# Two blocks of a bidirectional token mixer: who builds and sums the first two levels of a recurrence, and on how many rows and columns of TensorE

## The reference, cut to what matters

```python
scores = jnp.einsum('bhtsd,bhsd->bhts', qb[:, :, :, None, :] * decay, kb)   # decay = exp(cum_t - cum_s), s <= t
o = scores @ vb + (qb * jnp.exp(cum)) @ s
s_new = jnp.exp(last[:, :, 0, :])[..., None] * s + jnp.einsum('bhsd,bhse->bhde', kb * jnp.exp(last - cum), vb)
```

## Time and profile before

| | before |
| --- | --- |
| median of 3 runs | 3790.6 us (3789.75 to 3802.39) |
| the profiled execution | 3798.3 us, its span 3796.5 us |
| TensorE busy | 3503.6 us, 92% of the span |
| VectorE busy | 2010.7 us, 53% |
| ScalarE busy | 1149.5 us, 30% |
| mean granted TensorE clock | 0.965 |

### The profile page before, as it was taken

How to read it: one execution, slowest core, us unless ns; L and a number is a source line. 1 busy time by engine, 2 the same in 40 slices (tenths; PEclk the granted TensorE clock), 3 DMA queues, 4 the chain that set the end, 5 groups by cost and what they waited for, 6 DMA issues and landing times.

```text
span 3796.5 us, 50206 instructions
## 1 busy us (share of the span) xinstructions
PE 3503.6 (92%) x18584; PEld 2837.3 (75%) x18584; DVE 2010.7 (53%) x3025; ACT 1149.5 (30%) x1620; POOL 1003.3 (26%) x412
## 2 busy tenths in 40 slices
PE   6799999898889999999888889999999988989998
PEld 2388888787777777777677657788888767668887
DVE  5766341538844368783467575644331466762112
ACT  1221212344421123222433264321212332543222
POOL 2133223321121144444210101223223211123443
PEclk9899999999999999999989899999999988899999
DMA  5233332321132135453110101233322211112222
GB/s 197 94 125 129 123 111 78 132 67 34 40 107 64 52 116 174 172 174 107 62 67 23 56 17 34 99 111 133 122 103 66 77 40 34 45 44 84 94 94 94
DMA packets 101863, 341.46 MB, mean 90 GB/s; under 512 B 10159, under 2 KB 21551, under 8 KB 100240
## 3 DMA queue, kind: packets, MB, share of 16 engines
q1 hardware_dynamic: 82760, 301.90, 23.4%
q10 hardware_dynamic: 18952, 37.51, 2.8%
HBM read 325.21 MB, written 14.16 MB: 89 GB/s over the span
## 4 chain that ended last, share of the span: by engine, by line
issue 76%; POOL 19%; DMA 1%; PE 1%; DVE 1%; POOLq 0%; ACT 0%; ACTq 0%; SPq 0%; DVEq 0%
POOL wr_lo L2355 19%; PE ps L1259 1%; DMA raw<-in_stream 0%; DMA hyena_k<-fst 0%; PE ps L1266 0%; DVE mod_out L539 0%; DMA raw<-in_mod_stream 0%; PE ps L410 0%; POOLq L2354 0%; POOLq L2351 0%; DVE fnorm L1398 0%; ACTq L1319 0%; DVE H L740 0%; POOL wr_lo L2348 0%; PE ps L438 0%
## 5 line engine op out<-in xcount | busy, mean ns | idle before, releaser
L2355 POOL TENSOR_TENSOR wr_lo<-raw,wr_hi 128x1024 fp32r<-128x1024 f32 x388 | 970.0, 2504 | 2642.2 <-ACT wr_hi L494 2642.1
L410 PE MATMUL ps<-xx_hi,wr_hi 128*128 128x512 f32 x1728 | 689.1, 399 | 6.8 <-DVE H L900 5.7
L410 PE MATMUL ps<-xx_hi,wr_lo 128*128 128x512 f32 x1728 | 683.4, 395 | 0.0
L410 PE MATMUL ps<-xx_lo,wr_hi 128*128 128x512 f32 x1728 | 681.7, 395 | 0.0
L494 ACT ACTIVATE wr_hi<-raw 128x1024 fp32r<-128x1024 f32 x388 | 411.5, 1061 | 590.9 <-PE ps L410 309.0
L539 DVE CUSTOM_DVE_ANT_0 ps<-raw,cb 128x1024 f32<-128x1024 f32 x240 | 400.3, 1668 | 56.0 <-DMA raw<-in_mod_stream 25.8
L850 DVE TENSOR_TENSOR ff_raw<-ps,ff_gate 128x768 f32<-128x768 f32 (+1 forms) x88 | 72.6, 825 | 657.8 <-PE ps L410 650.3
L410 PEld LDWEIGHTS ps<-xx_hi,wr_hi 128*128 128x128 f32 x1728 | 326.6, 189 | 86.3 <-DVE H L900 6.5
L410 PEld LDWEIGHTS ps<-xx_lo,wr_hi 128*128 128x128 f32 x1728 | 326.6, 189 | 73.8 <-issue 2.1
L410 PEld LDWEIGHTS ps<-xx_hi,wr_lo 128*128 128x128 f32 x1728 | 326.3, 189 | 72.2
L900 DVE SCALAR_TENSOR_TENSOR H<-ps,hgv,H 128x512 f32 (+3 forms) x168 | 106.1, 659 | 285.5 <-PE ps L438 150.0
(11 more groups left out here) (383 smaller groups left out, 6193.9 us busy)
## 6 DMA issues: line engine op xcount, KB each, us to landing
raw<-in_stream SPq DMA_DIRECT2D x392, 512.0 KB, 3.3
raw<-in_mod_stream SPq DMA_DIRECT2D x168, 512.0 KB, 4.3
hK<-hyena_k ACTq DMA_DIRECT2D x4, 1152.0 KB, 6.0
h_kept<-H ACTq DMA_DIRECT2D x2, 2048.0 KB, 9.0
hyena_k<-fst ACTq DMA_DIRECT2D x14, 256.0 KB, 11.2
H<-in_h ACTq DMA_DIRECT2D x1, 3072.0 KB, 15.5
h_kept<-H ACTq DMA_DIRECT2D x1, 3072.0 KB, 9.9
H<-h_kept ACTq DMA_DIRECT2D x1, 3072.0 KB, 9.8
```

Source lines behind the costliest of these rows:

```text
L410: last = pe.matmul(gslot(slot)[:, col:col + n], w, rhs[part], start=(bi == 0 and pi == 0), stop=(bi == len(blocks) - 1 and pi == 2))
L2355: nc.gpsimd.tensor_tensor(wr_lo[:, s, :], raw[:, s % RAW, :], wr_hi[:, s, :], ALU.subtract).then_inc(tile_lo, 1)
```

## The change

ACT takes over the copies of levels 0 and 1 into `u_P`, block by block and with no mask: one copy of 64 key rows at level 0, two of 32 rows at level 1. ACT makes the copy of level li after its exponential of level li+2. DVE leaves out both masked copies and waits, before it copies level 2, for ACT's copy of level 1. At level 0 PE scores only the 64 key rows that are used. With two heads in a unit, the chunk sums (L968) become two products of 64 columns, one for each head, packed in 64 columns of features; the state `u_S` is 64 wide, its mask is gone, and the product with it in the output stage (L1003) reads the 64 feature rows of its own head. DVE waits for the `u_Z` of the level before, ahead of the exponents two levels on.

```diff
             for c in order[:5]:
-                last = pe.matmul(m[:, c * P:(c + 1) * P], U["ktok"][:, c * P:(c + 1) * P], vt(c),
-                                 start=True, stop=True)
+                for j in range(nsub):
+                    f = slice(j * P // nsub, (j + 1) * P // nsub)
+                    last = pe.matmul(m[f, c * P:c * P + P // nsub], U["ktok"][:, c * P + f.start:c * P + f.stop],
+                                     vt(c)[:, f], start=True, stop=True)
...
-                        last = pe.matmul(m[:, j * NX + c * HD:j * NX + (c + 1) * HD], Z[r, c * CH:(c + 1) * CH],
+                        keys = (slice(HD, P) if bw else slice(0, HD)) if li == 0 else slice(0, P)
+                        last = pe.matmul(m[keys, j * NX + c * HD:j * NX + (c + 1) * HD],
+                                         Z[r, c * CH + keys.start:c * CH + keys.stop],
                                          queries[r, c * per:(c + 1) * per, 0 if bw else 1, :], start=True, stop=True)
...
                     if at_order > 0:
-                        last = pe.matmul(m[f, cc], U["S"][:, at_order, f], U["eq"][:, cc], start=False, stop=True,
-                                         skip_group_check=True)
+                        last = pe.matmul(m[f, cc], U["S"][f, at_order, 0:P // nsub], U["eq"][f, cc],
+                                         start=False, stop=True, skip_group_check=True)
...
+        def act_put(act, tally, U, li, nsub, toks, ms, done, read):
+            b, bw, nch = LEVELS[li], U["bw"], toks // CH
+            act.wait_ge(misc_done, done)
+            for n in range(HD // b):
+                keys = slice((2 * n + bw) * b, (2 * n + bw + 1) * b)
+                queries = (2 * n + 1 - bw) * b
+                dst = U["P"].rearrange("p j (c t) -> p j c t", t=CH)[keys, :, :, queries:queries + b]
+                src = mslot(ms).rearrange("p (j c t) -> p j c t", j=2, t=HD)[keys, 0:nsub, 0:nch, n * b:(n + 1) * b]
+                ins = act.activation(dst, src, ACT.Copy)
+                if n < HD // b - 1:
+                    ins.then_inc(act_step, 1)
+                    act.wait_ge(act_step, tally.next("act_step"))
+            ins.then_inc(misc_free[ms], 1)
+            act.wait_ge(misc_free[ms], read)
...
+                if li in BLOCK_LEVELS:
+                    return
+                if li - 1 in BLOCK_LEVELS:
+                    dve.wait_ge(misc_free[tally.place("misc_done", 2)], tally.read("misc_done", 2))
...
-                src = add[:, c * P:(c + 1) * P]
-                if nsub == 2:
-                    src = U["Z"][:, 1, c * P:(c + 1) * P]
-                    dve.tensor_tensor(src, add[:, c * P:(c + 1) * P], blk[:, :], ALU.mult).then_inc(dve_step, 1)
-                    dve.wait_ge(dve_step, tally.next("dve_step"))
-                dst = U["S"][:, n_ + 1, :]
+                src = add[:, c * P:c * P + P // nsub]
+                dst = U["S"][:, n_ + 1, 0:P // nsub]
...
                 if li + 2 < nl:
+                    dve.wait_ge(z_ready, tally.now("z_ready", -2))
                     dve_seam(dve, tally, U, li + 2, toks)
```

More of the change, by code:

```diff
@@ L37 @@
 LEVELS = (64, 32, 16, 8, 4, 2, 1)
+BLOCK_LEVELS = (0, 1)
 RING = 4
@@ L1036, in act_unit @@
             tally.passed("misc_done", nsub + 1)
+            at_level = []
             for li in range(len(LEVELS)):
@@ L1039, in act_unit @@
                     act_level(act, tally, U, li, toks, scale)
-                tally.passed("misc_done")
+                at_level.append((tally.take("misc_done"), tally.now("misc_done"), tally.read("misc_done")))
+                if li - 2 in BLOCK_LEVELS:
+                    act_put(act, tally, U, li - 2, nsub, toks, *at_level[li - 2])
                 ahead(li)
             tally.passed("misc_done")
+        def act_put(act, tally, U, li, nsub, toks, ms, done, read):
[12 more added lines that the diff above has]
+            act.wait_ge(misc_free[ms], read)
         def dve_cum(dve, tally, U):
@@ L1143, in dve_unit @@
                 else:
-                    ins = dve.scalar_tensor_tensor(out=dst, in0=U["S"][:, n_, :], scalar=U["dec"][:, c:c + 1], in1=src,
+                    ins = dve.scalar_tensor_tensor(out=dst, in0=U["S"][:, n_, 0:P // nsub], scalar=U["dec"][:, c:c + 1], in1=src,
                                                    op0=ALU.mult, op1=ALU.add)
```

## The result

| | before | after |
| --- | --- | --- |
| median | 3795.9 us (4 runs, 3789.8 to 3802.4) | 3844.8 us (4 runs, 3839.2 to 3845.6) |
| the profiled execution, its span | 3796.5 us | 3843.8 us |
| mean granted TensorE clock | 0.965 | 0.954 |

The changed kernel is slower: the ratio is 1.0125, with a 95% interval of 1.0102 to 1.0149. The forecast was 3807 us (3771 to 3830).

The account below looks back on a forecast made before the run. TensorE, busy for 92% of the span, was taken as the bound. Row changes +36, waits -11.5, TensorE's own work -1.5 and clock -7 gave +16 us on 3790.6: 3807 us, range 3771 to 3830.

Parts of the forecast that it names:

- The price of a row change: Output stage: alternating 128*64 and 64*64 tiles cost 0.36 us per two instructions, 1.0 us more a chunk, 36 us in all.
- The first rival: Output stage: the two tile shapes take turns freely, with no drain, giving 3771 us; chance 0.17.
- The clock term: TensorE's clock dips behind the waits that the change removes would go too: 7 us off, 10 at most.
- The sign of being wrong: B units: the prediction is wrong if their mean clock moves by more than 0.05.
- The third rival: Behind unit ends: drains are paid and one or two more long low-clock stretches add 10 to 20 us, about 3825; chance 0.17.
- Waits ahead of level 1: B units: level 1's u_Z comes 1.9 us sooner, ending TensorE's waits there; all B-unit waits together 11.5 us off.
- ScalarE in A units: A units: ScalarE's level 0 copy delays its level 3 exponential, leaving VectorE 0.16 us gained instead of 0.9.
- the next step: A units: the 0.16 us gain is lost at GpSimd's subtraction, so 0 counted, between -7 and +3 us.
- TensorE's own work: Level 0 with half the weights and narrower chunk sums: 1.5 us off, from nothing to 5, over all units.

Follow-up runs that it names:

- second: The kernel before with one edit, the state product L1003 reading only its own head's 64 feature rows: 3857.3 us, ratio 1.0170.
- fourth: The kernel before with the second recurrence's output stage issued three times over, dense and of one tile shape: 3826.4 us, ratio 1.0094.
- seventh run: The kernel before with only ScalarE's copies of levels 0 and 1 and the 64 keys of level 0: 3790.1 us, ratio 0.9986.
- third run: The changed kernel with each chunk's u_P products of both heads before its u_S products, halving the row-size changes: 3794.6 us, ratio 1.0007.

## Why the prediction was wrong

**The price of a row change** was right. The step of two instructions was put at 0.36 us and measures 0.36 at 2.4 GHz, and so do its two parts: of the two in 0.43 us the last takes 0.27, so it starts 0.16 behind the first, which leaves 0.20 for the change. The 0.16 had no row behind it in the forecast, so that it fits is in part luck. At full clock the stage takes 7.7 us against 2.7 in the last unit of the first layer, 5.0 more for five chunks as counted, and 5.8 against 2.0 in that of the second, 3.8 more for four. The first rival (tiles that take turns freely) is out. By the rule that the section on the output stage cites from the Trainium skill ("TensorEngine Tiling (Array Packing)", Key Properties) the change from 128*64 to 64*64 drains the engine; the trace agrees, with 0.36 us for a run of two instructions where it was 0.11.

**The clock term failed**: "I count 7" off, with the opposite left to a rival of "one or two long stretches". The sign of being wrong that the prediction named for it came too: the mean clock of the second B unit moved by 0.14, where 0.05 was the mark. TensorE's busy time in the two stages can be read from windows, before and after:

```profile
1932.70:2119.33 186.63, 167.21 (x1404) 143.13 (x1404) 146.41 (x228) 54.31 (x65) 17.51 (x8) 0.89 0.07 23
3061.14:3213.89 152.75, 135.09 (x956) 107.65 (x956) 116.97 (x220) 47.24 (x65) 17.08 (x7) 0.84 0.08 28
```

```profile
1926.97:2148.77 221.80, 204.92 (x1444) 157.60 (x1444) 132.62 (x200) 61.41 (x77) 19.06 (x8) 0.77 0.06 22
3090.62:3259.75 169.13, 156.51 (x996) 111.72 (x996) 104.46 (x192) 52.62 (x77) 18.93 (x8) 0.76 0.08 26
```

Busy time goes from 302.3 to 361.4 us, 59 more. The row changes at full clock are 4 x 5.0 + 4 x 3.8 = 35 of it, and level 0 takes off 4 x 0.63 + 4 x 0.43 = 4. The remaining 28 us are put down to the lower clock. Idle time falls from 37.1 to 29.5 us. So the clock term was +28 and not -7. These 35 us are more than the whole distance of 31 between the forecast of +16 and the +47 of the two spans; the other terms together come to -3 (waits +4, row changes -1, level 0 -3, A units -4, in whole us). The prediction had seen that an output stage of scattered instructions might bring dips, but took as likelier that the dips would go with the waits. The second and fourth runs separate the two: the row changes alone bring the clock to 0.78 and 0.77, a dense stage of about the same length behind the same wait leaves it at 0.92 and 0.90. The third rival was the right case, and it was too small. Windows of the changed kernel, each around or behind one of the output stages and wholly at 1.2 GHz:

```profile
1973.00:1995.00 22.00, 21.08 (x115) 14.55 (x115) 8.07 (x17) 2.17 (x3) 2.34 (x1) 0.50 0.08 25
2028.00:2050.00 22.00, 21.08 (x115) 14.79 (x116) 8.66 (x18) 2.16 (x3) 2.10 (x1) 0.50 0.07 25
2083.00:2105.00 22.00, 21.08 (x115) 13.77 (x114) 6.76 (x14) 2.37 (x3) 2.34 (x1) 0.50 0.07 25
3125.00:3142.00 17.00, 16.61 (x87) 10.75 (x88) 5.87 (x16) 2.66 (x4) 2.34 (x1) 0.50 0.09 32
3165.00:3190.00 25.00, 24.01 (x119) 15.63 (x117) 10.53 (x26) 6.33 (x10) 2.34 (x1) 0.50 0.06 23
3213.00:3230.00 17.00, 16.61 (x88) 11.07 (x89) 6.48 (x18) 2.08 (x4) 2.34 (x1) 0.50 0.10 31
```

These six windows are 125 us together. The low stretches that they lie in are a little longer, 20.5 to 27.3 us and 140 us together. Before, such a long one (20.5 us) stood behind one unit (the second row). Not one or two more, but five.

How they begin is not the same everywhere. In the first two of the six units the clock fell 0.8 and 0.9 us into the stage. In the other four it had fallen 0.2 to 3.1 us ahead of the stage's first instruction, in the waits there. The kernel before had a fall at four of these six places too; three of the four lasted 3.4 us and one the 20.5. So the scattered stage costs mostly by how long the clock stays low, and less by new falls.

**Waits ahead of level 1** ended as said: no such row is left in any B unit of the changed kernel. The state chain takes 0.22 + 1.23 us with gaps, where some 1.5 were expected. In the last unit of the first layer the wait of 4.87 us, which is that of level 3, fell to 1.43. Level 5 waits 4.83 us instead of 0.75. TensorE's rows of levels 3 and 5 in the changed kernel:

```profile
2115.81 1.56 PE L987 MATMUL ps<-u_Z 64*128 64x64 f32 x24 [1.43 <-DVE u_Z L1131]
...
2129.32 2.79 PE L987 MATMUL ps<-u_Z 64*128 64x64 f32 x24 [4.83 <-DVE u_Z L1131]
```

And what stands ahead of level 5 on VectorE and GpSimd:

```profile
2121.23 3.56 DVE L2037 SCALAR_TENSOR_TENSOR cy<-cu,vecs,cy 128x512 f32<-128x512 f32 x2
...
2121.73 2.52 POOL L2380 TENSOR_TENSOR wr_lo<-raw,wr_hi 128x1024 fp32r<-128x1024 f32 x1 [35.59 <-ACT wr_hi L495]
```

The convolution's second half is ahead of level 5 in VectorE's order. The pair of `cy` takes 3.56 us there beside GpSimd's subtraction, and 1.54 in the first half (2110.73), so the subtraction costs 2.0 us. Before, one stood in the same stretch and cost 1.1 (a `u_Z` of 1.61 us instead of 0.55). TensorE ran its dense work between levels 3 and 5 at full clock and was there early. Before, it began that part at 1.2 GHz (24 instructions of level 3 in 2.75 us, 1.56 here) and came later, so that most of level 5's wait was covered. The wait moved on with the work; that is read from the rows, and no run tried it alone. It is where the waits fell short: the idle time of the first layer fell by 2.5 us where 6.9 were counted, that of the second by 5.0 where 4.6 were, all together by 7.6 where 11.5 were.

**ScalarE in A units.** The mechanism was right: ScalarE's exponential for level 3 is late now, and VectorE idles for it.

```profile
867.39 0.38 ACT L1061 ACTIVATE u_P<-ps 64x256 f32<-64x256 f32 x1
...
871.20 0.63 ACT L1029 ACTIVATE u_ex<-u_ex 128x512 f32<-128x512 f32 x1
...
871.93 0.42 DVE L1130 TENSOR_TENSOR u_Z<-u_ex,k1b 128x256 f32<-128x256 f32 x1 [0.77 <-ACT u_ex L1029]
```

The copy takes 0.38 us (0.39 forecast). From one output to that `u_Z` are 871.93 - 863.58 = 8.35 us, 8.46 before, so 0.11 gained there (0.16 forecast). What failed is the next step, that GpSimd's second subtraction would swallow it. The first subtraction starts later now and the second holds VectorE further on in its chain, in an instruction of 2.17 us instead of 2.62, and the unit is 0.7 us shorter. That is 3.6 us over the eight outputs (206.0 us apart, not 209.6), where 0 was forecast, within the bounds of -7 and +3. The seventh run, with these copies and their smaller level 0 alone, has the same 28.5 us a unit, so they are the cause; which step of the chain gives how much is read from the rows only.

**TensorE's own work** at level 0 fell by more than the 1.5 us taken: at full clock by 0.63 us in a wide B unit (0.92 for 1.55, in the seventh run), by 0.43 in one of 512 tokens and by 0.42 in an A unit (0.68 for 1.10). For all units that is 7.6 us, above the 5 allowed; the A units' part lies in a stage where TensorE has idle time. In three of the changed kernel's four wide units level 0 falls into a low stretch and takes 1.54 us, as long as before. The chunk sums of 20 narrow products take 1.33 us, as the 10 wide ones did (1.35).

## What to carry to other kernels

Count the changes of a matmul's row size in the order of issue before halving a contraction: with two instructions between changes each run cost 0.36 us where it had cost 0.11, and putting all products of one shape first turned a loss of 1.3% into a gain of 0.9% with the same instructions. Give the clock a term of its own, and ask how scattered the work behind a wait is: with a change of shape every 0.36 us TensorE was at 1.2 GHz for 20 to 27 us around each such stage of the changed kernel, and around dense stages of about the same length for 7 us at most. A narrower instruction on an engine that waits anyway moves the wait; look for the next late engine, as ScalarE was here, before counting what was taken from VectorE.

## What the runs showed of the hardware that was not expected

- A scattered stage behind idle time ran at 1.2 GHz, and the same stage with no idle time ahead of it at 2.4 (mean clock 0.53 and 1.00). Where the clock was not low already it fell 0.1 to 1.6 us into the stage (changed kernel, second and third run). In the first unit it then stayed at 1.2 GHz for another 12.5 us under dense work.
- The gap at a change of shape does not scale with the clock alone: the step of two instructions is 0.36 us at 2.4 GHz and 0.62 at 1.2.
- With two heads on separate column groups a step of four instructions costs 0.37 us, as much as one of two.
